# Moving the turned operands 64 bytes past their neighbours in SBUF, with 85 extra products whose results nobody reads

## The reference, cut to what matters

```python
h = rms_norm(x, g);  proj = h @ w_in                    # 1024 x 2496
x = x + concat(mla(proj), retention(proj)) @ w_out
x = x + memory_cross_attention(rms_norm(x, g), rms_norm(mem, g))
x = x + hierarchical_moe(rms_norm(x, g))                # 32 experts, two per token
# second block
z = rmsnorm(x) @ w_in_2                                 # 1024 x 7168, then RG-LRU and convolutions
x = x + merged @ w_out_2
x = x + (silu(g) * u) @ w_down_2                        # feed-forward of 2816
x = x + sigmoid(rmsnorm(x) @ w_ple_gate) * (p @ w_ple)
out = rmsnorm(x, g_final)
```

## Time and profile before

| | |
|---|---|
| median of 3 runs | 861.44 us (859.51 to 861.84) |
| the profiled execution | 858.64 us |
| its span, first to last instruction | 856.8 us |
| mean granted TensorE clock | 0.980 |
| TensorE matmul busy | 809.6 us (94%), 5562 matmuls |
| VectorE busy | 496.4 us |
| ScalarE busy | 416.3 us |
| DMA | 214.47 MB, mean 250 GB/s |

### The profile page before, as it was taken

How to read it: one execution, slowest core, us unless ns; L and a number is a source line. 1 busy time by engine, 2 the same in 40 slices (tenths; PEclk the granted TensorE clock), 3 DMA queues, 4 the chain that set the end, 5 groups by cost and what they waited for, 6 DMA issues and landing times.

```text
span 856.8 us, 13811 instructions
## 1 busy us (share of the span) xinstructions
PE 809.6 (94%) x5562; PEld 667.3 (78%) x5562; DVE 496.4 (58%) x835; ACT 416.3 (49%) x708; POOL 20.1 (2%) x41
## 2 busy tenths in 40 slices
PE   9999999999999877597979999999999999999996
PEld 7888888888865544244459999999988888888885
DVE  6667777856531210111168988888876555555486
ACT  5777488665411100000266757575746444444365
POOL 1600000000000000000000000000000000000000
PEclk9999999999999987899999999999999999999999
DMA  9855522978899999999975555555574665655421
GB/s 325 267 188 184 181 102 99 371 266 314 319 416 420 420 420 421 421 421 420 407 267 179 194 189 179 183 183 176 192 245 148 226 191 196 196 173 188 178 99 50
DMA packets 95184, 214.47 MB, mean 250 GB/s; under 512 B 4728, under 2 KB 59552, under 8 KB 81824
## 3 DMA queue, kind: packets, MB, share of 16 engines
q1 hardware_dynamic: 93456, 211.70, 67.8%
q0 software_dynamic: 1376, 1.89, 0.8%
q10 hardware_dynamic: 304, 0.20, 0.1%
HBM read 212.72 MB, written 1.05 MB: 249 GB/s over the span
## 4 chain that ended last, share of the span: by engine, by line
PE 79%; SPq 13%; DMA 4%; DVE 2%; ACT 1%; issue 1%; DVEq 0%; ACTq 0%
SPq L831 13%; PE bank L2244 13%; PE bank L2246 13%; PE bank L2245 13%; PE bank L3034 6%; PE bank L3035 6%; PE bank L3033 6%; PE bank L2261 4%; DMA over_queries<-in_expert_w_up_dram 3%; PE bank L2257 3%; PE bank L2754 3%; PE bank L2251 2%; PE bank L2252 2%; PE bank L2742 1%; PE bank L2787 1%; PE bank L2589 1%
## 5 line engine op out<-in xcount | busy, mean ns | idle before, releaser
L2244 PE MATMUL bank<-w_hi,xT_hi 128*128 128x512 f32 (+2 forms) x390 | 150.8, 387 | 0.0
L2246 PE MATMUL bank<-w_hi,xT_lo 128*128 128x512 f32 (+2 forms) x390 | 148.4, 381 | 0.0
L2245 PE MATMUL bank<-w_lo,xT_hi 128*128 128x512 f32 (+2 forms) x390 | 148.2, 380 | 0.0
L3033 PE MATMUL bank<-hT_hi,w_hi 128*128 128x256 f32 x440 | 124.6, 283 | 0.0
L3034 PE MATMUL bank<-hT_lo,w_hi 128*128 128x256 f32 x440 | 124.5, 283 | 0.0
L3035 PE MATMUL bank<-hT_hi,w_lo 128*128 128x256 f32 x440 | 124.5, 283 | 0.0
L452 DVE TENSOR_TENSOR w_lo<-stage,w_hi 128x1024 fp32r<-128x1024 f32 (+3 forms) x78 | 87.8, 1126 | 31.7 <-ACT w_hi L438 30.8
L438 ACT ACTIVATE w_hi<-stage 128x1024 fp32r<-128x1024 f32 (+3 forms) x80 | 78.6, 983 | 27.7 <-PE bank L2246 13.3
L454 DVE TENSOR_TENSOR w_lo<-stage,w_hi 128x1024 fp32r<-128x1024 f32 (+3 forms) x78 | 87.5, 1122 | 0.0
L3034 PEld LDWEIGHTS bank<-hT_lo,w_hi 128*128 128x128 f32 x440 | 84.5, 192 | 0.0
L3035 PEld LDWEIGHTS bank<-hT_hi,w_lo 128*128 128x128 f32 x440 | 84.5, 192 | 0.0
(11 more groups left out here) (505 smaller groups left out, 1660.8 us busy)
## 6 DMA issues: line engine op xcount, KB each, us to landing
stage<-in_w_in_dram SPq DMA_DIRECT2D x36, 1024.0 KB, 5.1
stage<-in_w_gate_up_dram SPq DMA_DIRECT2D x44, 512.0 KB, 4.7
stage<-in_w_down_dram SPq DMA_DIRECT2D x11, 1024.0 KB, 4.8
whole<-in_expert_w_up_dram SPq DMA_DIRECT2D x10, 1024.0 KB, 25.4
stage<-in_w_out_dram SPq DMA_DIRECT2D x8, 1024.0 KB, 5.1
whole<-in_expert_w_gate_dram SPq DMA_DIRECT2D x8, 1024.0 KB, 23.4
stage<-in_cross_w_kv_dram SPq DMA_DIRECT2D x7, 1024.0 KB, 8.8
stage<-in_expert_w_gate_dram SPq DMA_DIRECT2D x7, 1024.0 KB, 13.0
```

The source lines that it names most:

```text
L2244: mm(o, k_hi, v_hi, start=start, stop=False)
L2245: mm(o, k_hi, v_lo, start=False, stop=False)
L2246: return mm(o, k_lo, v_hi, start=False, stop=stop)
L3033: mm(o, w_hi[:, s, at:at + P], hT_hi[:, k, :], start=k == 0, stop=False)
```

## The change

The diff does two things. It moves tiles in SBUF. And it has TensorE make 85 extra float32r products.

The tiles: 64 bytes of nothing stand ahead of `xT`, `aT` and `cT`. Small fillers behind `turned_unit`, `const` and the small vectors move all that follows, and `token_gates` changes places with two small tiles, which now lie over `biased` and `exps`. Worked out as above, after the change `xT`, `aT`, `cT`, `rx`, `hT` and the other recurrent tiles start at 64 modulo 128 bytes. `stage`, `w_hi`, `w_lo`, `whole`, `x`, `xs`, `y_hi`, `y_lo`, `turned_unit` and `const` keep theirs at 0. `spent_unit`, `hidden`, `token_now`, `hiddenT`, `arena`, `embed`, all the `over_*`, `raw_turned`, `slot_of` and `xg` start at 0.

The products: `unread` multiplies 128 columns of `y_hi` by 512 columns of `y_lo` into `bank[4]`, each product starting a new sum, so that nobody reads the result. A pair (s, m) moves the start of the stationary and of the moving operand by so many words of 4 bytes; each pair is done five times. `in_quad` stands between the turned slots and the up columns of quads 1 to 4 (3, 3, 3 and 2 pairs). `behind` stands after the way back of quads 1 and 2 (3 pairs each). That makes 17 pairs.

```diff
-    turned_memory, (xT_hi, xT_lo, aT_hi, aT_lo, cT_hi, cT_lo) = parts(
-        ("xT_hi", [P, KD, 2 * P], F32R), ("xT_lo", [P, KD, 2 * P], F32R), ("aT_hi", [P, 2, 2 * P], F32R),
+    turned_memory, (_, xT_hi, xT_lo, aT_hi, aT_lo, cT_hi, cT_lo) = parts(
+        ("turned_apart", [P, 16], F32), ("xT_hi", [P, KD, 2 * P], F32R), ("xT_lo", [P, KD, 2 * P], F32R), ("aT_hi", [P, 2, 2 * P], F32R),
...
     turned_unit = sb("turned_unit", [P, SLOT])
+    sb("turned_end", [P, 32])
...
     const = sb("const", [P, KEPT_COLS])
+    sb("spent_apart", [P, 24])
...
+    sb("hidden_apart", [P, 24])
...
-    hot_rank = eb("hot_rank", [P, T, EXPERTS])
+    hot_rank, left_gates = biased[:, :, 0:EXPERTS], exps[:, :, 0:EXPERTS]
...
-    left_gates = eb("left_gates", [P, T, EXPERTS])
...
-    eb("unused2", [P, 74])
+    token_gates = eb("token_gates", [P, T, EXPERTS, 2])
+    eb("unused2", [P, 58])
...
-    token_gates = eb("token_gates", [P, T, EXPERTS, 2])
...
+        still, moved = (y[:].rearrange("p c n -> p (c n)") for y in (y_hi, y_lo))
+        in_quad = {1: ((0, 0), (16, 0), (0, 16)), 2: ((0, 0), (8, 0), (0, 8)), 3: ((0, 0), (4, 0), (0, 4)), 4: ((0, 0), (16, 16))}
+        behind = {1: ((0, 0), (24, 0), (0, 24)), 2: ((0, 0), (8, 16), (16, 8))}
+
+        def unread(words):
+
+            for s, m in words:
+                for n in range(5):
+                    mm(bank[4][:, :], still[:, s:s + P], moved[:, m:m + 512], start=True, stop=True)
+
         def quad(q):
 
             columns(q, 0)
             turn_slots(q)
+            unread(in_quad.get(q, ()))
             if q == QUADS - 1:
                 turn_sums()
             columns(q, 1)
...
             bring_back(q)
+            unread(behind.get(q, ()))
             if q == QUADS - 3:
                 add_tokens()
```

More of the change, by code:

```diff
@@ L763, in first_slots @@
             fill_slots(0, ranks)
-            nc.vector.tensor_copy(hot_rank[:], ranks)
+            nc.vector.tensor_copy(hot_rank, ranks)
         def keep_counts():
@@ L2002, in _ @@
         with dve.If(over_flag > 0):
-            stt(left_gates[:], hot_rank[:], OWN + STRIP - 0.5, token_gates[:, :, :, 0], ALU.is_gt, ALU.mult)
+            stt(left_gates, hot_rank, OWN + STRIP - 0.5, token_gates[:, :, :, 0], ALU.is_gt, ALU.mult)
             dve.wait_ge(sem("over_blocks"), KD)
```

## The result

The changed kernel took 865.70 us (median of 6 runs, 863.77 to 870.37), the kernel before 860.94 us (6 runs, 858.68 to 862.97). The ratio is 1.0073 with a 95% interval of 1.0053 to 1.0093: slower, by 4.8 us between the medians and 6.3 us by the ratio, where I had forecast no change. Its profiled execution took 865.94 us.

A forecast was written before the change was run, and what follows sets the result against it. Bound by float32r products outside the quads and the weight stream from quad 3 on. 858.6 us profiled + 0 for the products + 0 for the places = 858.6, or 861.4 us as median; range 854 to 869 us.

The forecast's parts named there:

- no change: Whole kernel: likeliest case, time within 0.3% (2.6 us) of the kernel before; chance 64 in 100.
- What bounds the kernel: Whole kernel: float32r products outside the quads, the weight stream from quad 3 on, earlier TensorE work only if that stream ran dry.
- The extra products at 0 us: Quads 1 to 4: 85 products take 19.3 us of TensorE time, hidden by the weight stream, so 0 us.
- The places at 0 ns a product: Products with moved operands: 3,148, 1,732 with moving weights and 1,416 with moving hT or rx, keep their pace.
- rival C: Moved operands: the offset hurts, 1 to 2.5 ns on 3,148 products, some 866 us; chance 11 in 100.
- pairs that differ by 64: token_now with y_*, starts 64 apart modulo 128: read at 120 and 235 ns, like pairs at 0, hence 0 ns.
- The bound: Moved operands, dear side: 2.5 ns more on all 3,148 products, 7.9 us, kept as 8 us either side.
- 448-column rows: Latents' products with varying moving starts: 202.5 ns each, 15.8 over 186.7, so 2.5 more than the others.
- A: Moved operands: the offset removes most of the extra, 10.4 ns on 3,148 products, 33 us, 828 us; chance 3 in 100.
- B: Moved operands: the offset helps a little, 1 to 2.5 ns on 3,148 products, some 856 us; chance 15 in 100.
- D: Weight stream: late releases empty the DMA queue or hold SyncE; full price 19.3 us, likelier some 5, 866 us; 7 in 100.

The follow-up runs named there:

- e1: Kernel before plus the 85 unread products, places of before: 859.83 us (12 runs), ratio 1.0000.
- e5: Kernel before plus 600 unread products in quad 1, 24 for each fixed pair of start places, 512 and 256 columns; only gaps counted, 226.7 and 120.0 ns level.
- e2: Changed kernel without the unread products, all tile moves kept: 865.51 us (6 runs), ratio 1.0062 to the kernel before.
- e3: Kernel before with only xT, aT and cT moved by 64 bytes and everything behind by 128: 866.75 us (6 runs), ratio 1.0079.
- e4: Kernel before with only rx, hT and the recurrent tiles between and behind moved by 64 bytes: 856.87 us (12 runs), ratio 0.9966.
- e6: Kernel before with xT, aT, cT, rx and hT 64 bytes below the weights' place modulo 256: 852.46 us (one run).
- e8: Kernel before with xT, aT, cT 32 and hT 96 bytes above the weights' place modulo 256: 868.58 us (one run).
- e11: Kernel before with 40 words of filler ahead of rx, putting rx and hT 96 bytes below the weights' place modulo 256: 857.77 us (one run).
- e13: Kernel before plus 432 products in quad 1, sums of one product or 24, finer map of starts; one run, only gaps counted: 113.3 ns at 64 below, 256 columns.
- e9: Kernel before with 192 bytes of filler ahead of rx, putting rx and hT 64 bytes below the weights' place modulo 256: 850.71 us (4 runs), ratio 0.9887.
- e12: Kernel before plus 288 products of 256 columns in quad 1, starts fixed or walking by 512 bytes; one run, only gaps counted: 117.7 or 117.8 ns at 64 below.
- e7: Kernel before with xT 128 bytes from the weights' place modulo 256, aT and cT level, hT 32 above: 864.03 us (one run).

## Why the prediction was wrong, point by point

**What bounds the kernel** was read rightly: split products outside the quads, the weight stream inside. That is also why the pace of the split products went straight into the time.

**The extra products at 0 us: right.** The last of the 15 behind quad 1 end at 286.19 us, where quad 2's gates start; before they started at 275.76 us. Of these 10.4 us, 3.5 are older than the experts and 6.9 are the products, against 6.8 forecast. e1 shows the term by itself, at a ratio of 1.0000, and by the first gate product of each quad its lateness went as forecast: 6.7 us at quad 2, 13.7 at quad 3, 6.1 at quad 4 and -0.1 at quad 5, where I had 6.8, 13.6, 7.4 and 0.6. From quad 3 on the weight stream sets the time again. In the changed kernel the clock stays at 1.00 from 311.30 to 357.10 us, which are quads 3 and 4, where it had been at 0.88 and 0.83. That earlier quads ran at a higher clock brought the end no nearer: the last quad's up columns start within 0.1 us of before in e1.

**The places at 0 ns a product: this step failed.** The term was 3,148 products by 0 ns. By the settled paces it should have been 1,732 by +6.7 and 1,416 by -2.2 ns: +11.6 and -3.1, 8.5 us at most. Measured in the trace are 7.3, and 4.8 between the medians. The trace shows where the difference lies. Of the products with moving weights only 1,620 have 512 columns (the rest 256 to 448), and from start to start they take 6.0 ns more on average, 9.7 us in all, as those near a switch of shape gain less. The others and the transposes between them take 0.6 us less. The heads take 2.35 us less and not 3.1, since they begin with more products at the half clock in this execution:

```profile
441.79:446.79 5.00, 5.00 (x32) 4.84 (x33) 4.75 (x8) 4.90 (x9) 0.00 (x0) 0.84 0.18 55
445.78:450.78 5.00, 5.00 (x25) 4.77 (x26) 3.87 (x7) 3.80 (x6) 0.00 (x0) 0.66 0.19 56
```

(The heads' first 5 us, before and changed: 32 products at a mean clock of 0.84 against 25 at 0.66. e1, with the places of before, has this late clock too, so it is not an effect of the places.) The half microsecond of the quads makes up the rest. I had named the pair of starts as what matters and had counted the groups nearly rightly, and I had a rival C on the right side with 11 in 100. The failure is in the sentence "So I take 0 ns a product", and it has three parts.

First, the comparison was coarser than the effect. The earlier trace rows were read to 10 ns over two to four products soon after a switch of shape. Some patterns of e5 settle only after ten or so, and what was to be found was 2 to 7 ns. The three from 67.22 to 67.92 us are 229, 232 and 231 ns by their starts, and it is the long stream behind them that runs at 226.7.

Second, I compared the wrong relation. I had "pairs that differ by 64" and did not ask in which direction, nor modulo what. `token_now` lies 64 below `y_*` modulo 256. With it moving, that is the 64-below case, which the change does not give the heads; with it stationary, it is the 64-above case of 512 columns (229), where the change makes the 64-below one (233.3).

Third, the trace of before did hold a sign of the effect. By their starts, the first four of line 2824, at 433.12 us, come at 195, 116 and 114 ns, and the next form 114 ns behind them. That looks like the beginning of the 113.3 pattern. I took the y_lo four at 434.12, whose 480 ns include a switch, and read 120. By their starts they come at 117, 117 and 119 ns, and the 128 ns to the next form are the switch.

**The bound** of 2.5 ns, from the 448-column rows, was too small: those rows have level starts too (a block of 448 columns is 1,792 bytes, seven times 256) and say nothing of other ones. With 6.7 ns for the 1,732 the range would have been wider on the dear side. The measured 865.7 us lies inside 854 to 869, but only because the range was wide enough for a loss that I had not forecast: I had said no change, and the places cost 0.6% alone (e2) and 0.7% in the changed kernel.

**The rivals.** A falls: in none of the pairs measured do 512 columns come under 226.6 ns, which is 10.6 over the 216 that the earlier trace rows show for float32 records. The Trainium skill (TensorE: Matmul & The Clock Gate, Back-to-back issue gap) gives N / 2.4 + 2.5 ns as the gap of an isolated product, which is 215.8 for 512 columns, and about 131 ns for a stream with a weight load before each product. No stream of such float32r products here comes under 226.6. My forecast had put that section's formula down to a stream. B and C both happened in part: the 256-column products gained 2.2 ns, inside B's 1 to 2.5, and the 512-column ones lost 6.7, beyond C's; each had been priced on all 3,148. D did not happen: the stream carried 415 to 423 GB/s from slice 12 to 19.

**What is not settled.** Shown is that the difference of the two start places changes the pace: e3 and e4 each by one half, e5 and e6 to e8 by many values. Not every difference has one pace of its own: for 256 columns, 64 below has two, and 96 below gave 117.3, 118.7 and 120.0 ns in e5, e11 and e13. Why it does is not shown. That both operands are read from SBUF at the same time, and that their reads meet more or less often depending on the difference, fits all of it but was not measured. Nor is it known what picks 113.3 or 117.8 ns at 64 below; in the heads of e6 and e9 it was 113.3 throughout, and the four runs of e9 lie within 1 us. The chip alone does not pick it, since e9 with 113.3 and e12 with 117.8 ran on the same one. The changed kernel also has products of 256 columns at this difference, 96 with `xT` stationary and the weights moving, and they take 117.7 ns in their longer streams.

## What to carry to other kernels

When a float32r product takes more than its columns explain, look at where the stationary and the moving operand start, modulo 256 bytes. Try the moving one 64 bytes below for 256 columns, and level for 512, and measure, as these were the best of the places tried in this one kernel. One filler tile in front of the activations was worth 1.1% here, and moving `xT` alone cost 0.8% (e3). And before a cost is called zero by comparison, compare streams long enough to settle, in the same relation and direction, at a resolution finer than the bound divided by the count.

## What the runs showed of the hardware that I had not expected

- Float32r products in a steady stream: 512 columns 226.6 to 227.0 ns with level starts, 228.9 to 234.5 with others; 256 columns 120.0 ns level, 113.3 at best with the moving operand 64 bytes below.
- The best place for one width is nearly the worst for the other: level starts are best for 512 columns, and for 256 no settled stream that was measured lies over them by more than 0.1 ns.
- 128 bytes of shift are not neutral: `hT` at 118.7 in place of 120.0 ns in e3, `xT` at 232.5 in place of 226.7 ns in e7.
- The same instruction on the same addresses, 256 columns at 64 below, ran at 117.8 ns in two kernels (e5, e12) and at 113.3 in a third (e13).
